# A fused decoder layer in fp32: the down projection of its MLP by seven block products for eight, half of the weight sums made by GpSimd

## The chip, the core and the metric

The kernel runs on one NeuronCore of one Trainium2 chip. The metric is the device time of one execution in microseconds; the kernel before takes 2036.14 us (median of 3 runs, 2035.08 to 2038.41). The profile holds one execution. TensorE (PE) multiplies and writes to PSUM; VectorE (DVE), ScalarE (ACT) and GpSimd (POOL) compute elementwise; SyncE (SP) issues most DMAs.

## The reference, cut to what matters

One layer of a hybrid decoder (attention beside a Mamba scan, then an MLP) for 256 tokens of width 2048, all in fp32. The change is in the MLP:

```
D_MODEL = 2048; SEQ = 256; D_FF = 4 * D_MODEL
        hn = rms_norm(h, norm_mlp_w[l])
        h = h + jnp.square(jax.nn.relu(hn @ w_up[l])) @ w_down[l]
    return rms_norm(h, norm_final_w)
```

## The kernel before, in words

**Precision.** Every large product is made of fp32r products: a weight block `raw` is split into a high part `hi` (a copy to fp32r) and a low part `lo = raw - hi`; the activations are split likewise (`LAh`/`LAl`, `LBh`/`LBl`). A block product is three matmuls of 512 columns: high by high, high by low, low by high (lines 307 to 309).

**Tiles.** Weights come in tiles of 256 rows of depth by 512 columns, so two 128x512 blocks, 512 KB in one DMA. A *chunk* is 512 output columns: 8 tiles over a depth of 2048, and for both halves of the tokens (t = 0, 1) 8 x 2 x 2 x 3 = 96 matmuls into two PSUM banks `acc[par][t]`, `par` alternating from chunk to chunk. One tile is 12 matmuls.

**The ring.** `raw`, `hi` and `lo` are rings of 4 slots (`RING`). In `load_group`, SP loads tile g once `lo` of tile g-4 is made. In `split_hi` ScalarE makes `hi` once the tile has landed and TensorE is through with tile g-4; in `split_lo` VectorE makes `lo` from it; TensorE waits for `lo` in `mm_group`. `slots` sets the order on ScalarE and VectorE: at slot s they split tile s+3 (`LEAD`), then do what is hooked to slot s. All engines work in order.

**The MLP** runs in 4 phases. Phase i makes four up chunks (columns of `w_up`; product, relu, square; transposed on VectorE by `turn_blocks`, spread by four DMAs that GpSimd issues in `spread_blocks`, and split into `LAh`/`LAl` by `act_split_s` and `dve_split_s` 4 slots after the chunk's end), and then multiplies these 2048 hidden values by a quarter of `w_down` in four down chunks, each added to the residual `H` by `add_residual`. So a phase is 64 tiles, and the MLP 256. The last chunk (`mm_last`) does its second half token half by token half, and the final norm follows: row sums, the power -1/2 on GpSimd (line 814), scaling on VectorE and ScalarE, four output DMAs.

Of the kernel before, what the change touches and what calls it, by code (L numbers as in the profile page):

```python
# [22 lines left out]
F32 = mybir.dt.float32  # L23
F32R = mybir.dt.float32r
# [7 lines left out]
P = 128  # L32
# [41 lines left out]
C_END = C_MLP + 32  # L74
# [21 lines left out]
def build(nc, a, out):  # L96
    ctx = ExitStack()
    with ctx:
# [60 lines left out]
        s_x0 = sem("first_rows_of_x_split")  # L159
        s_smw = sem("small_weights_landed")  # L160
# [81 lines left out]
        s_fr = sem("final_rsqrt_ready")  # L242
        s_fin = [[sem(f"output_ready{t}{n}") for n in range(2)] for t in range(2)]
        s_wf = sem("final_weights_landed")
        s_out = sem("output_stored")

# [50 lines left out]
        def mm_group(pe, g, par, j, Lh, Ll, n=NC):  # L297

            sl = g % RING if isinstance(g, int) else j % RING
            pe.wait_ge(s_lo, g + 1)  # L300
            for kk in range(2):
                k = 2 * j + kk
                for t in range(2):
# [213 lines left out]
        XDT = sb("XDT", [P, 2, NC], c=post)  # L517
# [4 lines left out]
        ZT = sb("ZT", [P, 2, NC], c=post)  # L522
        TB = sb("TB", [P, 2 * NC], c=post)
        YT = sb("YT", [P, NC], c=post)
        TS = W[:, 0:4, :, :].rearrange("p h c l -> p (h c l)")
        TSS = (TS, XTOK[:, :, :].rearrange("p t n -> p (t n)"))
        TBS = (TB[:, :], W[:, 4:8, :, :].rearrange("p h c l -> p (h c l)"))
        post.close()
        flat_th = TH.rearrange("p a s -> p (a s)")
# [21 lines left out]
        PART = ((slice(0, 1024), slice(1024, D)), (slice(0, 1280), slice(1280, D)))  # L551
# [8 lines left out]
        def _(sp):  # L560
# [4 lines left out]
            load_group(sp, C_KC, 0, w_in, 0, KC0)  # L565
            load_x(1)
            load_group(sp, C_KC, 1, w_in, 0, KC0)
# [3 lines left out]
            load_group(sp, C_KC, 4, w_in, 0, KC0)  # L571
            load_x(3)
            for j in (5, 6, 7):
                load_group(sp, C_KC, j, w_in, 0, KC0)
# [32 lines left out]
            with sp.Fori(0, 4) as i:  # L607
                for k in range(4):
                    load_chunk(sp, C_MLP + 8 * i + k, w_up, 0, D * i + NC * k)
                for k in range(4):  # L610
                    load_chunk(sp, C_MLP + 8 * i + 4 + k, w_dn, KT * i, NC * k)
            for t, n in ((0, 1), (0, 0), (1, 0)):
                sp.wait_ge(s_fin[t][n], 1)
                sp.dma_start(out_rows[:, t, PART[t][n]], GB[:, t, PART[t][n]]).then_inc(s_out, 16)
            sp.wait_ge(s_out, 64)
# [3 lines left out]
        def _(pool):  # L619
# [10 lines left out]
            pool.memset(identf[:, :], 0.0)  # L630
            pool.memset(zz[:, :], 0.0)
# [10 lines left out]
            pool.drain()  # L642
            pool.affine_select(identf[:, :], identf[:, :], [[-1, P]], ALU.not_equal, 1.0, base=0, channel_multiplier=1)
# [174 lines left out]
        def _(pe):  # L818
            pe.wait_ge(s_const, 1)
# [1156 lines left out]
```

## Time and profile before

| | |
|---|---|
| median of 3 runs | 2036.14 us |
| the profiled execution's own time | 2037.86 us |
| its span, first to last instruction | 2036.1 us |
| TensorE busy | 2018.9 us (99%) |
| VectorE / ScalarE / GpSimd busy | 68% / 51% / 14% |
| mean granted TensorE clock | 0.998 |
| read from HBM | 379.91 MB |

A matmul's record is longer than its share of the time, since matmuls are pipelined: what one costs is the time of a busy stretch divided by their number. "Idle before <-X" tells what ended an engine's idle time.

### The profile page before, as it was taken

How to read it: one execution, taken by the hardware profiler on the slowest of the kernel's cores; microseconds unless marked ns; L12 is line 12 of the kernel's file. 1: busy time of each engine (PE TensorE's matmuls, PEld its weight loads, DVE VectorE, ACT ScalarE, POOL GpSimd, SP SyncE). 2: the span in 40 equal slices, each digit the busy share in tenths (PEclk: the TensorE clock that was granted, in tenths of full speed). 3: DMA queues.
4: the chain of work that ended last, by engine and by line, in shares of the span. 5: the costliest groups of instructions: out<-in, count | busy, mean ns of one | idle time of the engine just before them, and what ended most of it. 6: DMA issues, size and time to landing. Idle time of an engine off the chain costs nothing.

```text
span 2036.1 us, 26601 instructions
## 1 busy us (share of the span) xinstructions
PE 2018.9 (99%) x9378; PEld 1666.9 (82%) x9378; DVE 1384.1 (68%) x1735; ACT 1034.7 (51%) x1454; POOL 278.6 (14%) x417
## 2 busy tenths in 40 slices
PE   9999999999999999999999999999999999999997
PEld 7888888888888877888887888888888888888886
DVE  6665878687665678885688877666556556655664
ACT  5444546464544567663566644544344434433443
POOL 4000111111110233330033311011001000000000
PEclk9999999999999999999999999999999999999999
DMA  8757666666666666666666677766666666666663
GB/s 274 219 178 208 195 194 191 195 192 192 175 208 208 183 191 198 193 197 209 183 185 185 194 255 233 229 211 204 215 195 203 223 197 193 221 205 185 219 216 135
DMA packets 202726, 411.49 MB, mean 202 GB/s; under 512 B 15264, under 2 KB 15360, under 8 KB 201200
## 3 DMA queue, kind: packets, MB, share of 16 engines
q1 hardware_dynamic: 188656, 364.56, 58.0%
q0 software_dynamic: 13776, 44.96, 7.6%
q8 instruction: 74, 1.21, 0.3%
q14 instruction: 44, 0.36, 0.1%
q10 hardware_dynamic: 176, 0.40, 0.1%
HBM read 379.91 MB, written 2.16 MB: 188 GB/s over the span
## 4 chain that ended last, share of the span: by engine, by line
PE 91%; DVE 3%; ACT 2%; issue 2%; ACTq 1%; DVEq 0%; POOLq 0%; POOL 0%; DMA 0%
PE acc L307 28%; PE acc L309 28%; PE acc L308 28%; DVE lo L274 1%; PE x L999 1%; ACT hi L268 1%; ACT W L1313 1%; PE tr L948 1%; PE tr L342 1%; PE x L931 1%; DVE XCT L1697 0%; PE x L937 0%; PE x L867 0%; ACTq L1314 0%; PE tr L950 0%
## 5 line engine op out<-in xcount | busy, mean ns | idle before, releaser
L274 DVE TENSOR_TENSOR lo<-raw,hi 128x1024 fp32r<-128x1024 f32 x688 | 837.8, 1233 | 457.9 <-ACT hi L268 450.0
L268 ACT ACTIVATE hi<-raw 128x1024 fp32r<-128x1024 f32 x688 | 718.8, 1057 | 623.3 <-PE acc L309 561.4
L307 PE MATMUL acc<-hi,LAh 128*128 128x512 f32 x1840 | 727.9, 396 | 0.0
L309 PE MATMUL acc<-hi,LAl 128*128 128x512 f32 x1840 | 717.3, 390 | 0.0
L308 PE MATMUL acc<-lo,LAh 128*128 128x512 f32 x1840 | 716.6, 389 | 0.0
L307 PEld LDWEIGHTS acc<-hi,LAh 128*128 128x128 f32 x1840 | 345.5, 188 | 75.3 <-issue 3.2
L309 PEld LDWEIGHTS acc<-hi,LAl 128*128 128x128 f32 x1840 | 345.3, 188 | 73.1
L308 PEld LDWEIGHTS acc<-lo,LAh 128*128 128x128 f32 x1840 | 345.6, 188 | 70.6 <-issue 1.1
L307 PE MATMUL acc<-hi,LBh 128*128 128x512 f32 x896 | 349.8, 390 | 0.0
L309 PE MATMUL acc<-hi,LBl 128*128 128x512 f32 x896 | 348.7, 389 | 0.0
L308 PE MATMUL acc<-lo,LBh 128*128 128x512 f32 x896 | 348.6, 389 | 0.0
L307 PEld LDWEIGHTS acc<-hi,LBh 128*128 128x128 f32 x896 | 168.2, 188 | 35.1 <-DVE lo L274 0.3
L309 PEld LDWEIGHTS acc<-hi,LBl 128*128 128x128 f32 x896 | 168.2, 188 | 35.0
L308 PEld LDWEIGHTS acc<-lo,LBh 128*128 128x128 f32 x896 | 168.2, 188 | 34.8
L390 POOL DMA_DIRECT2D W<-TB x48 | 26.0, 560 | 491.6 <-DVE TB L381 491.6
L1697 DVE SCALAR_TENSOR_TENSOR XCT<-XCT,CWs 128x255 f32<-128x255 f32 (+2 forms) x144 | 59.8, 477 | 0.0
L769 POOL TENSOR_TENSOR ZT<-ZT,XR 128x512 f32<-128x512 f32 x32 | 56.4, 1780 | 17.9 <-ACT ZT L1300 13.9
L390 POOL DMA_DIRECT2D XTOK<-W x48 | 26.0, 558 | 219.9 <-DVE W L381 219.9
L1211 ACT ACTIVATE PB<-x,NM 128x256 f32<-128x256 f32 (+1 forms) x64 | 26.0, 420 | 38.1 <-DVE SCB L1640 27.1
L1105 ACT ACTIVATE XR<-acc,RSX 128x512 f32<-128x512 f32 x28 | 19.3, 690 | 47.9 <-PE acc L309 46.2
L762 POOL DMA_DIRECT2D XCT<-TB x32 | 18.0, 572 | 166.2 <-DVE TB L1812 166.2
L1313 ACT ACTIVATE W<-W,NAs 128x128 f32<-128x128 f32 x128 | 39.0, 388 | 0.0
(343 smaller groups left out, 1324.4 us busy)
## 6 DMA issues: line engine op xcount, KB each, us to landing
raw<-w_in SPq DMA_DIRECT2D x304, 512.0 KB, 4.3
raw<-w_up SPq DMA_DIRECT2D x128, 512.0 KB, 3.9
raw<-w_down SPq DMA_DIRECT2D x128, 512.0 KB, 4.8
raw<-w_proj_ssm SPq DMA_DIRECT2D x64, 512.0 KB, 4.7
raw<-w_proj_nsa SPq DMA_DIRECT2D x32, 512.0 KB, 4.7
raw<-w_out SPq DMA_DIRECT2D x32, 512.0 KB, 5.5
W<-acs_rows POOLq DMA_DIRECT2D x8, 1024.0 KB, 6.7
W<-TB POOLq DMA_DIRECT2D x48, 128.0 KB, 4.1
```

Of the source, the lines that this page charges most:

```text
L268: act.activation(hi[:, sl, :, :], raw[:, sl, :, :], ACT.Copy).then_inc(s_hi, 1)
L274: dve.tensor_tensor(lo[:, sl, :, :], raw[:, sl, :, :], hi[:, sl, :, :].bitcast(F32), ALU.subtract).then_inc(s_lo, 1)
L307: pe.matmul(o, xh, wh, start=(k == 0), stop=False)
L308: pe.matmul(o, xh, wl, start=False, stop=False)
L309: x = pe.matmul(o, xl, wh, start=False, stop=(k == KT - 1))
L342: x = pe.transpose((banks or TR)[b][:, (ct % 2) * S + t * P:(ct % 2) * S + (t + 1) * P], src[:, t, ct * P:(ct + 1) * P], identf[:, :])
L390: eng.dma_start(TSS[n % 2][:, S * a:S * (a + 1)], TBS[n % 2][32 * a:32 * (a + 1), :].rearrange("i (b n) -> i b n", b=4)).then_inc(s_sp[n % ...
L769: pool.tensor_tensor(ZT[:, t, :], ZT[:, t, :], ZR[:, t, :], op)
L931: pe.matmul(X6[:, :], Q[:, n, P:S], K[:, :, 0:2 * P].rearrange("p k (b n) -> p b k n", b=2), start=(p_ == 0), stop=(p_ == 2), skip_group_c ...
L1211: act.activation(o, src, ACT.Exp, scale=SCALE, bias=NM[:, k:k + 1], accum_out=SUM[:, k:k + 1])
L1313: act.activation(W[:, h, c, :], W[:, h, c, :], ACT.Relu, bias=NAs[:, c, h:h + 1], scale=-1.0)
L1697: dve.scalar_tensor_tensor(XC[:, ct, k:S], TH[:, ct, 0:S - k], CWs[:, 3 - k, ct:ct + 1], XC[:, ct, k:S], ALU.mult, ALU.add)
```

## The change

**The seven products.** The change takes two neighbouring down chunks (c, c+1) together, with the two token halves and two neighbouring 128-row blocks of depth. That is a 2x2 by 2x2 block product, made by seven block products for eight from sums of blocks (Winograd's form of Strassen's scheme). It does so on the first four depth blocks, two units (u = 0, 1), of each chunk pair: in both pairs of phases 0 to 2 and in the first pair of phase 3, 7 pairs and 14 units. The rest stays as it was.

**The tiles of a unit.** `a` is the tile of chunk c, `b` that of chunk c+1. Two more tiles are not loaded but made in ring slots: `p` = (b0-a0, b1-b0) by VectorE, and `q` = (p1+a0, a1-q0) by GpSimd (`later_weight_sums`). All four are split into `hi` and `lo` (of `b` only the second block). TensorE does 2, 1, 2 and 2 block products on them, 21 matmuls where 24 were. A pair of chunks is 20 tiles in `QUAD_ORDER`: four plain tiles (depth 2 to 5) of chunk c, a b p q of unit 0, two plain tiles, a b p q of unit 1, six plain tiles of chunk c+1. Four products go to PSUM banks of their own (`B1`, `B5`, `B6`, `B7`), which VectorE adds up in five steps hooked to tiles 13 to 17. Per phase VectorE also makes four sums of activation blocks (`row_sums`), which ScalarE and VectorE split.

**Waits.** SP loads into the slot of an `a` or `p` only when GpSimd's sums of that unit are made (`s_wq`). VectorE makes `p` when `a` and `b` have landed. The loops over phases are written out.

**Start and tail.** The identity is made first, TensorE starts on it earlier, the first tile is split by halves, the loads of x and of the first tiles are in another order, and `turn_x(1)` stands after the first tile's matmuls. In the tail the power -1/2 is a square root on ScalarE, then a reciprocal, one Newton step and a product on VectorE, and rows t = 1 go out in four DMAs for two.

```
+QUAD_ORDER = ([("n", 0, j) for j in (2, 3, 4, 5)] + [(c, 0, 0) for c in "abpq"] + [("n", 0, j) for j in (6, 7)] +
+              [(c, 0, 1) for c in "abpq"] + [("n", 1, j) for j in (2, 3, 4, 5, 6, 7)])
...
+            def load_tile(sp, i, x):
...
+                kind, c, j, _ = tile_of(i, x)
+                if kind in "pq":
+                    return
+                sp.wait_ge(s_lo, G_MLP + PHASE * i + x - RING + 1)
+                before, _, u, _ = tile_of(i, x - RING) if x >= RING else ("n", 0, 0, 0)
+                if before in "ap":
+                    sp.wait_ge(s_wq, 4 * i + 2 * ((x - RING - UP) // QUAD) + u + 1)
...
+            def later_weight_sums(i, q, u):
...
+                pool.wait_ge(s_lo, g)
+                pool.wait_ge(s_raw[sa], 16 * (2 * C_MLP + 16 * i + tile_of(i, x)[3]))
+                pool.wait_ge(s_wt, 4 * i + 2 * q + u + 1)
+                pool.tensor_tensor(raw[:, sq, 0, :], raw[:, sp_, 1, :], raw[:, sa, 0, :], ALU.add)
+                pool.drain()
+                pool.tensor_tensor(raw[:, sq, 1, :], raw[:, sa, 1, :], raw[:, sq, 0, :], ALU.subtract).then_inc(s_wq, 1)
...
+            def seven_products(g, u, p0, p1):
...
+                pe.wait_ge(s_lo, g + 1)
+                product(B1, *rows(0, 0), g, 0, one, two)
+                product(acc[p0][0], *rows(0, 1), g, 1, False, two).then_inc(s_mm, 1)
+                pe.wait_ge(s_lo, g + 2)
+                product(acc[p1][0], *sums(4), g + 1, 1, one, False).then_inc(s_mm, 1)
+                pe.wait_ge(s_lo, g + 3)
+                product(B5, *sums(1), g + 2, 0, one, two)
+                product(B7, *sums(3), g + 2, 1, one, two).then_inc(s_mm, 1)
+                pe.wait_ge(s_lo, g + 4)
+                product(B6, *sums(2), g + 3, 0, one, two)
+                product(acc[p0][1], *rows(1, 1), g + 3, 1, False, two).then_inc(s_mm, 1)
...
+            def split_tile(i, x):
...
+                if kind in "pq":
+                    act.wait_ge(s_wt if kind == "p" else s_wq, 4 * i + 2 * ((x - UP) // QUAD) + u + 1)
+                else:
+                    act.wait_ge(s_raw[sl], 16 * (2 * C_MLP + 16 * i + loads))
+                act.wait_ge(s_mm, g - RING + 1)
+                k0 = 1 if kind == "b" else 0
+                act.activation(hi[:, sl, k0:2, :], raw[:, sl, k0:2, :], ACT.Copy).then_inc(s_hi, 1)
...
+                if kind == "a":
+                    dve.wait_ge(s_lo, g - 1)
+                    for n in (sa, sb_):
+                        dve.wait_ge(s_raw[n], 16 * (2 * C_MLP + 16 * i + tile_of(i, x + (n == sb_))[3]))
+                    for kk, (m, mk) in enumerate(((sa, 0), (sb_, 0))):
+                        y = dve.tensor_tensor(raw[:, sp_, kk, :], raw[:, sb_, kk, :], raw[:, m, mk, :], ALU.subtract)
+                    y.then_inc(s_wt, 1)
+                dve.wait_ge(s_hi, g + 1)
```

**The order on VectorE** in the down projection of phase 0. Before, from the split of the last up chunk's values (L415) on; `lo<-raw,hi` is the low part of a tile, L1872 adds a chunk to the residual:

```order
L415 TENSOR_TENSOR LAl<-XTOK,LAh 128x1024
L274 TENSOR_TENSOR lo<-raw,hi 128x1024 x4
L1872 TENSOR_TENSOR BCT<-acc,BCT 128x512 x2
L274 TENSOR_TENSOR lo<-raw,hi 128x1024 x8
L1872 TENSOR_TENSOR BCT<-acc,BCT 128x512 x2
```

In the changed kernel the second chunk pair reads so up to its unit 1 and its first steps of adding up (L2113 makes `p`, the 128x512 row is `b`, `tr` and `x` are the added banks):

```order
L2113 TENSOR_TENSOR raw<-raw 128x512 x2
L2117 TENSOR_TENSOR lo<-raw,hi 128x1024
L2117 TENSOR_TENSOR lo<-raw,hi 128x512
L2117 TENSOR_TENSOR lo<-raw,hi 128x1024 x4
L2113 TENSOR_TENSOR raw<-raw 128x512 x2
L2117 TENSOR_TENSOR lo<-raw,hi 128x1024
L2117 TENSOR_TENSOR lo<-raw,hi 128x512
L2117 TENSOR_TENSOR lo<-raw,hi 128x1024 x5
L2141 TENSOR_TENSOR BCT<-acc,BCT 128x512 x2
L2117 TENSOR_TENSOR lo<-raw,hi 128x1024
L2148 TENSOR_TENSOR BCT<-tr,BCT 128x512
```

The sums of `p` stand in front of the low part of `a`, and between the two units are only p, q and two plain tiles.

**The order on GpSimd**, changed kernel, at the end of a phase's spreads; before, each spread was followed by the next one:

```order
L426 DMA XTOK<-W 128x1x256 [waits event_read_by_dve,blocks_turned]
L426 DMA XTOK<-W 128x1x256 x3
L881 TENSOR_TENSOR raw<-raw 128x512 [waits weight_sums_made,raw0,lo_done]
L883 TENSOR_TENSOR raw<-raw 128x512
L881 TENSOR_TENSOR raw<-raw 128x512 [waits weight_sums_made,raw2,lo_done]
L883 TENSOR_TENSOR raw<-raw 128x512
```

**The order on SP**, changed kernel, the second chunk pair of a phase; before, each load waited for `lo_done` alone. The waits for GpSimd's sums (`later_weight_sums_made`) stand at the loads into the slots of `a` and `p`, and the loads behind them are held back too:

```order
L666 DMA raw<-w_down 128x2x512 [waits lo_done] x9
L666 DMA raw<-w_down 128x2x512 [waits later_weight_sums_made,lo_done]
L666 DMA raw<-w_down 128x2x512 [waits lo_done]
L666 DMA raw<-w_down 128x2x512 [waits later_weight_sums_made,lo_done]
L666 DMA raw<-w_down 128x2x512 [waits lo_done]
L666 DMA raw<-w_down 128x2x512 [waits later_weight_sums_made,lo_done]
L666 DMA raw<-w_down 128x2x512 [waits lo_done]
L666 DMA raw<-w_down 128x2x512 [waits later_weight_sums_made,lo_done]
```

Over the whole program TensorE's matmuls of 512 columns go from 8320 to 8278, which is 42 fewer, 3 for each of the 14 units.

## Rows read from the trace of the kernel before

**Rows 1.** The page: span and engines; busy us (share) xinstructions.
```profile
span 2036.1 us, 26601 instructions
...
PE 2018.9 (99%) x9378; PEld 1666.9 (82%) x9378; DVE 1384.1 (68%) x1735; ACT 1034.7 (51%) x1454; POOL 278.6 (14%) x417
```

**Rows 2.** Busy time by stretch, two MLP phases and more (us, PE, PEld, DVE, ACT, POOL, clock).
```profile
1600.00:2000.00 400.00, 400.00 (x1766) 331.23 (x1765) 233.96 (x211) 170.32 (x172) 17.33 (x32) 1.00 0.66 207
```

**Rows 3.** Waits from 1600 us on: who for whom, total us, times, longest.
```profile
ACT hi L268 <- PE acc L309: 179.9, 117, 2.0
```

**Rows 4.** Timeline in a down projection, start and length in us; then its loads.
```profile
1800.55 1.23 DVE L274 TENSOR_TENSOR lo<-raw,hi 128x1024 fp32r<-128x1024 f32 x1 [1.50 <-ACT hi L268]
...
1801.94 27.57 SPq L255 DMA_DIRECT2D raw<-w_down  x11
1801.98 0.39 PE L307 MATMUL acc<-hi,LAh 128*128 128x512 f32 x1
...
1802.18 1.06 ACT L268 ACTIVATE hi<-raw 128x1024 fp32r<-128x1024 f32 x1 [1.66 <-PE acc L309]
...
1803.27 1.23 DVE L274 TENSOR_TENSOR lo<-raw,hi 128x1024 fp32r<-128x1024 f32 x1 [1.49 <-ACT hi L268]
...
DMA to landing us min/median/max: 4.5/4.5/4.9
```

**Rows 5.** Loads of `raw`: 400 us, then a single one after an idle queue.
```profile
DMA to landing us min/median/max: 3.5/4.6/8.1
...
DMA to landing us min/median/max: 3.7/3.7/3.7
```

**Rows 6.** Group by form: a sum of two 128x512 operands on VectorE.
```profile
L1788 DVE TENSOR_TENSOR Y<-Y,XDT 128x512 f32<-128x512 f32 x8 | 5.5, 693 | 0.6
```

**Rows 7.** GpSimd sums of 128x512 (ns min/median/max), and VectorE beside two pairs.
```profile
L769 POOL TENSOR_TENSOR ZT<-ZT,XR x32: 1292/1742/2280, 702.4 to 1157.6; 128x512 f32<-128x512 f32 x32
...
909.55 3.53 POOL L769 TENSOR_TENSOR ZT<-ZT,XR 128x512 f32<-128x512 f32 x2 [1.79 <-ACT ZT L1300]
913.58 3.97 POOL L769 TENSOR_TENSOR ZT<-ZT,XR 128x512 f32<-128x512 f32 x2 [0.50 <-issue]
...
L274 DVE TENSOR_TENSOR lo<-raw,hi x3: 2311/2317/2317, 911.8 to 916.3; 128x1024 fp32r<-128x1024 f32 x3
```

**Rows 8.** Timeline from the end of an up projection, per engine.
```profile
1894.72 0.69 ACT L1105 ACTIVATE XR<-acc,RS 128x512 f32<-128x512 f32 x1 [1.66 <-PE acc L309]
...
1906.84 1.06 ACT L405 ACTIVATE LAh<-XTOK 128x1024 fp32r<-128x1024 f32 x1 [2.91 <-DMA XTOK<-W]
...
1909.08 2.35 DVE L274 TENSOR_TENSOR lo<-raw,hi 128x1024 fp32r<-128x1024 f32 x2
```

**Rows 9.** Timeline of the start.
```profile
4.42 2.18 PE L897 MATMUL x<-identf 128*128 128x128 f32 x9
...
6.39 1.91 PE L342 MATMUL tr<-identf,GA 128*128 128x128 f32 x8
...
9.17 1.65 PE L342 MATMUL acc<-identf,GA 128*128 128x128 f32 x8
...
10.74 0.47 PE L307 MATMUL acc<-hi,LAh 128*128 128x512 f32 x1
...
13.57 1.04 PE L342 MATMUL tr<-identf,GA 128*128 128x128 f32 x8
```

**Rows 10.** Timeline of the tail, and a one-column operation on ScalarE.
```profile
2026.93 0.15 DVE L1938 TENSOR_SCALAR VV<-SS 128x1 f32<-128x1 f32 x1
2027.75 0.89 DVE L1947 TENSOR_SCALAR GB<-GB,RS 128x1280 f32<-128x1280 f32 x1 [0.67 <-POOL RS L814]
...
4.18 0.20 ACT L1115 ACTIVATE SS<-mhalf 128x1 f32<-128x1 f32 x1 [1.59 <-POOLq L654]
```

**Rows 11.** Stretches behind the last matmul: the third number from the end is the granted clock.
```profile
2025.30:2027.69 2.39, 0.00 (x0) 0.00 (x0) 1.61 (x4) 0.73 (x2) 0.52 (x1) 1.00 0.72 290
2027.70:2036.00 8.30, 0.00 (x0) 0.00 (x0) 0.89 (x1) 0.94 (x1) 0.02 (x1) 0.50 0.32 127
```

More of the change, by code:

```diff
@@ L73, with tile_of @@
 C_END = C_MLP + 32
-C_END = C_MLP + 32
+UP, QUAD, TWO = 32, 20, 16
+PHASE = UP + 2 * QUAD
+G_MLP = 8 * C_MLP
+G_END = G_MLP + 3 * PHASE + UP + QUAD + TWO
+QUAD_ORDER = ([("n", 0, j) for j in (2, 3, 4, 5)] + [(c, 0, 0) for c in "abpq"] + [("n", 0, j) for j in (6, 7)] +
+              [(c, 0, 1) for c in "abpq"] + [("n", 1, j) for j in (2, 3, 4, 5, 6, 7)])
+TWO_ORDER = [("n", c, j) for c in range(2) for j in range(8)]
+def tile_of(i, x):
+    if x < UP:
+        return "n", x // 8, x % 8, x // 4 + 1
+    q, y = divmod(x - UP, QUAD)
+    order = TWO_ORDER if (q == 1 and i is LAST) else QUAD_ORDER
+    kind, c, j = order[y]
+    loads = UP // 4 + 4 * q + sum(order[z][0] not in "pq" for z in range(y % 4, y + 1, 4))
+    return kind, 4 + 2 * q + (c if kind == "n" else 0), j, loads
+LAST = 3
 E_U, E_KC, E_VC, E_AT = 0, 4, 5, 6
@@ L570, in _ @@
             load_group(sp, C_KC, 3, w_in, 0, KC0)
[L571 removed]
             load_x(3)
[L573 removed]
+            for j in (4, 5, 6, 7):
                 load_group(sp, C_KC, j, w_in, 0, KC0)
@@ new lines, in mlp_chunk, with product @@
+            def mlp_chunk(g, par, Lh, Ll, need):
+                for j in range(8):
+                    for (se, v) in need.get(j, ()):
+                        pe.wait_ge(se, v)
+                    mlp_group(g + j, par, j, Lh, Ll, t_first=(j == 0, j == 0), last=(j == 7))
+            def product(o, xh, xl, g, kk, start, stop):
+                sl = g % RING
+                pe.matmul(o[:, :], xh, hi[:, sl, kk, :], start=start, stop=False)
+                pe.matmul(o[:, :], xh, lo[:, sl, kk, :], start=False, stop=False)
+                return pe.matmul(o[:, :], xl, hi[:, sl, kk, :], start=False, stop=stop)
@@ L1397, in mlp @@
                 if first:
                     hk[4] = [lambda: act_split_s(act, 7, LBh, 12, COLS[:, CN2 + 12:CN2 + 16])]
-                slots(act, split_hi, C, 64, hk, last)
+                phase_slots(i, hk)
             mlp(0, first=True)
-            with act.Fori(1, 3) as i:
+            for i in range(1, 3):
                 mlp(i)
-            mlp(3, last=True)
+            act.wait_ge(s_v, 1)
+            act.activation(RSX[:, 2:3], VV[:, 0:1], ACT.Sqrt)
+            mlp(LAST)
             for t in range(2):
```

322 lines of the change are left out of this document (251 added, 71 removed).

## The prediction, made before the changed kernel had run

> **What bounds the kernel now.** I read the page's head and its table of busy time first: TensorE is busy for 2018.9 of 2036.1 us [rows 1]. The view by stretch shows the same for the MLP: 400.00 us busy in 400 us at a granted clock of 1.00, the upper of its two levels (2.4 GHz), with 1766 matmuls, so 0.2265 us each and 2.72 us for a tile of 12 [rows 2]. The list of waits says who runs ahead: ScalarE, which makes the high parts, waited 179.9 us for TensorE to free a ring slot [rows 3]. So the suppliers have slack, and a matmul less is 0.2265 us less, for as long as they keep it.
>
> Then the timeline, for the loop of a ring slot, which is what the change works on. TensorE begins its next tile at 1801.98; the slot it left is rewritten from 1802.18 by ScalarE (0.20 us later), and VectorE's low part starts at 1803.27 (1.09 later). For the slot before, the low part starts at 1800.55 and SP issues the next load at 1801.94 (1.39 later). That load lands 4.5 us on [rows 4]. So SP issues a load 0.20 + 1.09 + 1.39 = 2.7 us after TensorE left the slot, and it lands at 7.2. It is wanted at 11.1, when TensorE has done the four tiles of the ring (10.9) and ScalarE comes round to the slot: 3.9 us to spare.
>
> **What is removed.** 42 matmuls x 0.2265 = 9.5 us [rows 2], all on the path.
>
> **What is added beside it.** VectorE adds up the four product banks: from product tile 13 on it has nine operations of 0.69 at the most, which follow each other every 0.61 (the slot length of back-to-back ones, as two sums next to each other in the unit below), and one of 1.14, 6.6 us, beside five low parts at 1.14, 5.7 us; with drains some 13 us, where TensorE takes 5 x 2.72 = 13.6. It starts with three tiles ready. I cost it, and the four activation sums per phase, at nothing; the cover is those three tiles, 8.2 us, and beyond them it costs microsecond for microsecond. ScalarE has over a microsecond idle per tile. The unrolled loops add no wait that I can see.
>
> **What is added in a chain.** This is the term that decides. In a unit two of the four slots hold sums, so loads come late. Let A be the moment when TensorE starts on tile `a` of unit 0. It then has 21 matmuls, two plain tiles (24) and 21 matmuls: 66 x 0.2265 = 14.95 us until it wants the first plain tile of chunk c+1, and 60 (13.6 us) until `q` of unit 1. The suppliers:
> 1. Slot of the last plain tile before `a` is free at A. `q` of unit 0 gets its high part from A+0.20, its low part from A+1.29, and `b` of unit 1, whose slot it is, is issued at A+2.7 [rows 4].
> 2. It lands 4.5 us later, A+7.2 [rows 4].
> 3. VectorE, next in line, makes `p`: two sums of 0.69, 1.3 together [rows 6]: A+8.5.
> 4. GpSimd makes `q` in two sums. Alone one takes 1.29; behind a low part 2.27 or so; the median is 1.74, and a drain between them costs 0.50. Two such pairs took 3.53 and 3.97, and low parts beside them 2.32 for 1.23 [rows 7]. Each engine waits out the other's operation. I take 4.1, nearest to a first sum behind `a`'s low part (2.3), the drain (0.5) and a second alone (1.3): A+12.6.
> 5. High and low part of `q`, 1.09 + 1.28: A+14.95. TensorE wanted it at 13.6: 1.4 us late.
> 6. SP, held by GpSimd's sums, issues the next plain tile at A+12.75. The queue is idle then, where a load took 3.7; in the busy queue it took 4.6 in the median [rows 5]. I take 4.0: A+16.75. High and low part, 2.37: A+19.1.
> TensorE wanted that tile at 14.95, so it has stood still for 4.15 us in all.
>
> In the first pair of each phase it is worse. ScalarE and VectorE must split the last up chunk's values at tile 3 of the pair, ahead of `q`. The chunk ends 0.20 before 1894.72, at 1894.52; ScalarE waits for the spread values until 1906.84, and the next low part starts only at 1909.08 [rows 8]. A is 48 matmuls after the chunk's end, 1905.39, so the load of step 1 goes out at 1909.08 + 1.39 = A+5.1 instead of A+2.7: 2.4 us more, 6.55.
>
> So four first pairs lose 26.2 us and three second pairs 12.5: 38.7, less 9.5 saved, **+29.1 us**. GpSimd's part is 4.1 of a pair's chain. A sum of two such operands takes VectorE 0.69 [rows 6]: two, with a drain, would be 1.4, and 2.7 us a pair, 19 us in all, would not be lost. The Trainium skill (GPSIMD Engine Reference, Engine selection) speaks against the change here: it puts elementwise sums on VectorE, with GpSimd about twice as slow for two inputs. By its factor alone the pair of sums would take some 2.8 us and a drain, 3.3, and the result would be 6 us less; I stay with the rows, which show the two engines waiting for each other.
>
> **Start and tail.** The transposes of x start at 6.39 behind a warm-up that could end a microsecond earlier, and the first product is at 10.74; but a second block of transposes, hidden before at 9.17, now stands between products, where such a block costs 1.04 [rows 9]. I take 0.5 us saved, between 1.8 saved and 0.8 lost. In the tail the variance's start to scaling is 2026.93 to 2027.75, 0.82 us. After the variance's own 0.15 come now a root on ScalarE (0.20) and four one-column steps on VectorE at 0.15 and a drain each, some 0.7 us more [rows 10]; the last DMAs are smaller, which I take to give 0.2 back: 0.5 lost, between 0.3 saved and 1.0 lost. Together nothing.
>
> **The sum.** 2037.9 (the profiled execution, 1.7 over the median shown) + 29.1 = 2067; the median gives 2036.1 + 29.1 = **2065**.
>
> **Bounds.** Below: both loads at the shortest seen, 3.5 [rows 5], and GpSimd without meeting VectorE, 1.29 + 0.50 + 1.29 = 3.1, give 1.0 + 0.5 + 1.0 = 2.5 less a pair, 17.5 us in all: 2047.6. Above: both loads at 4.9 [rows 4] and 4.5 for GpSimd (3.97 + 0.50) give 1.7 more a pair, 12 us, and start and tail 1.8: 2079.
>
> **Rivals.**
> *The clock falls in the new gaps.* For: TensorE's gap before the plain tile is 2.7 us (16.4 to 19.1), and after the last matmul the clock stayed at 1.00 for 2.4 us and then went to 0.50, the lower level (1.2 GHz) [rows 11]. At the start the work ran at the lower level from 4.42 until past 9.17: eight transposes took 1.91 at 6.39, 1.65 at 9.17 and 1.04 at 13.57 [rows 9]. Such a stretch of 5 to 6 us at half speed costs 3, in 7 pairs 21: 2086. Against: 2.7 us is just about what the tail shows without a fall, and the gap is surrounded by full work. The Trainium skill (TensorE: Matmul & The Clock Gate, HAM oscillation) describes just this, waits for data between bursts that bring the lower clock back every time; by it the time would be that 2086.
> *VectorE becomes the bound while adding up.* If its nine operations take 1.0 for 0.69 and drains add up, it falls behind its three tiles of cover; 2 us a pair, 14 us: 2079. Against: 8 us of cover.
> *The chain fits, and it is faster.* If steps 1 to 6 end within 14.95 us, no stall is left and 9.5 us are gained: 2026.6. It turns to a gain below a chain of 16.3 (9.5 / 7 = 1.36 us of stall a pair), 2.8 us under my 19.1. For: a load has 3.9 us to spare before the change. Against: even the lower bounds of steps 2, 4 and 6 together give 16.6 in the second pairs, and 2.4 more in the first. A run near 16.3 would be no change.
> That the change does not do what it says is ruled out by the order of instructions: 42 matmuls are gone.
>
> **The chances.** My forecast 0.72 (its own range 2048 to 2079), the clock 0.10, VectorE 0.06, no stall 0.08, near balance 0.04. The 8 in 10 range goes from the lower bound towards the first two rivals: 2047 to 2082. A measurement of this kernel tells 0.2%, 4 us, from no change: faster by more 0.08, within 0.04, slower by more 0.88.
>
> **What would show it.** TensorE's idle time in the down projections, about 39 us, in gaps before `q` and before the first plain tile behind unit 1, ended by the low parts (L2117). VectorE waiting for a landing before L2113. GpSimd's pairs L881/L883 taking about 4 us, and the load waiting on them. A clock of 1.00 throughout. Wrong would be: no gaps there; gaps at the adding up; gaps at unit 0's `q` alone; or a clock of 0.50 behind them.

## The result, and the profile after

The changed kernel takes 2082.69 us in the median of four runs (2079.52 to 2084.47), the kernel before 2036.39 beside it: a ratio of 1.0225 with a 95% interval of 1.0213 to 1.0238, so 46.3 us slower. The forecast was 2065, so +29.1, with a range that ended at 2082: the sign was right, and the size was missed by 17 us. One execution of run 1 below took 4483.6 us, over twice as long as any other, and is left out. The profiled execution took 2082.11 us. Its page, against [rows 1]:

```profile
span 2080.4 us, 25990 instructions
...
PE 2028.5 (98%) x9351; PEld 1665.8 (80%) x9351; DVE 1498.1 (72%) x1877; ACT 1066.2 (51%) x1492; POOL 332.7 (16%) x443
```

The span grew by 44.3 us. TensorE is busy for longer than before although 42 matmuls are gone, which points to matmuls at the lower clock. The view by stretch shows them: the first row is the 600 us that answer to [rows 2], where before no idle time was shown; the others are the five stretches of the MLP at the lower level (us, busy us and instructions of PE, PEld, DVE, ACT and POOL, granted clock, DMA share, GB/s).

```profile
1400.00:2000.00 600.00, 565.52 (x2423) 459.38 (x2422) 430.14 (x414) 263.64 (x263) 81.25 (x82) 0.98 0.60 190
```

```profile
1435.30:1445.50 10.20, 8.07 (x18) 5.93 (x19) 6.69 (x7) 3.81 (x4) 2.04 (x1) 0.50 0.57 203
1500.20:1503.60 3.40, 3.13 (x7) 2.51 (x8) 3.06 (x4) 2.41 (x3) 0.00 (x0) 0.50 0.84 276
1626.50:1629.90 3.40, 3.40 (x10) 2.66 (x9) 2.82 (x4) 1.48 (x2) 0.79 (x1) 0.51 0.04 13
1687.90:1691.30 3.40, 3.40 (x10) 2.62 (x9) 2.90 (x4) 1.85 (x3) 0.00 (x0) 0.50 0.98 304
1998.50:2001.90 3.40, 3.40 (x10) 2.66 (x9) 2.99 (x5) 1.09 (x2) 1.16 (x1) 0.50 0.02 6
```

TensorE stands idle for 34.5 of these 600 us. In the five stretches matmuls start 0.427 apart where they otherwise start 0.2265 apart, as here in the third:

```profile
1627.16 0.63 PE L1167 MATMUL acc<-lo,LAh 128*128 128x512 f32 x1
1627.58 0.63 PE L1168 MATMUL acc<-hi,LAl 128*128 128x512 f32 x1
```

49 matmuls begin inside them (the 55 in the rows count those that reach into a stretch too), each 0.20 longer: 9.8 us for the clock. The list of waits of TensorE from 1400 us to the end (who for whom, us in total, times, longest) says what it waits for, and two more rows of that list what stands behind it; before, TensorE had no such wait, and ScalarE's longest entry was [rows 3]:

```profile
PE acc L1166 <- DVE lo L2117: 23.6, 13, 2.6
PE tr L1181 <- DVE lo L2117: 8.9, 4, 3.9
PE x L1181 <- DVE lo L2117: 3.0, 4, 1.3
...
ACT hi L1549 <- POOL raw L883: 24.7, 8, 5.0
...
POOL raw L883 <- issue: 8.8, 4, 4.3
```

`acc L1166` is the first plain tile behind a unit, `tr L1181` is the product with `q` of unit 0, `x L1181` a product with `p`. A matmul is shown with 0.39 but the next may follow after 0.2265, so a gap from start to start is 0.16 longer than its idle time. Counted from start to start, and without the clock's part, the gaps in the MLP add up to 42.4 us; my forecast had 38.7.

One first pair in full, phase 1, from the timeline (start, length, engine, line, idle before and its releaser). Tile `a` of unit 0 starts at A = 1616.3: the chunk ends 0.20 before the ACT row below, and four plain tiles, 10.9, follow.

```profile
1605.64 0.69 ACT L1537 ACTIVATE XR<-acc,RS 128x512 f32<-128x512 f32 x1 [1.66 <-PE acc L1168]
...
1610.88 2.17 POOL L426 DMA_DIRECT2D XTOK<-W  x4 [19.59 <-DVE W L417]
...
1611.62 1.28 DVE L2113 TENSOR_TENSOR raw<-raw 128x512 f32<-128x512 f32 x2
```

```profile
1613.07 2.71 POOL L881 TENSOR_TENSOR raw<-raw 128x512 f32<-128x512 f32 x1
...
1617.26 1.90 POOL L883 TENSOR_TENSOR raw<-raw 128x512 f32<-128x512 f32 x1 [1.48 <-issue]
1619.19 1.06 ACT L1549 ACTIVATE hi<-raw 128x1024 fp32r<-128x1024 f32 x1 [2.69 <-POOL raw L883]
1619.23 0.88 SPq L666 DMA_DIRECT2D raw<-w_down  x2
...
1621.56 0.51 PE L1181 MATMUL tr<-hi,LSh 128*128 128x512 f32 x1 [1.68 <-DVE lo L2117]
...
1625.84 0.47 PE L1166 MATMUL acc<-hi,LAh 128*128 128x512 f32 x1 [2.61 <-DVE lo L2117]
```

```profile
1627.64 1.29 DVE L2113 TENSOR_TENSOR raw<-raw 128x512 f32<-128x512 f32 x2 [0.58 <-DMA raw<-w_down]
...
1629.11 2.11 POOL L881 TENSOR_TENSOR raw<-raw 128x512 f32<-128x512 f32 x1 [9.95 <-DVE raw L2113]
...
1631.37 1.56 POOL L883 TENSOR_TENSOR raw<-raw 128x512 f32<-128x512 f32 x1
1633.00 0.37 SPq L666 DMA_DIRECT2D raw<-w_down  x1
```

```profile
1639.37 0.50 PE L1166 MATMUL acc<-hi,LAh 128*128 128x512 f32 x1 [1.34 <-DVE lo L2117]
```

Three things are to be seen. GpSimd's pair in unit 1 takes from 1628.93, the end of VectorE's sums, to 1632.93: 4.0 us. In unit 0, right behind the DMAs that spread the last up chunk's values, the first sum is 2.71, then GpSimd waits 1.48 for nothing that the profile shows (4.33 in phase 0), and from the end of VectorE's sums at 1612.90 it is 6.26 us. And SP issues no load at all between 1603.54 and 1619.23: the first of the next four, into the slot of `a`, waits for GpSimd, and the other three queue behind it. Their landings, from that line's own view for 1619 to 1622 us:

```profile
L666 SPq DMA_DIRECT2D raw<-w_down x4: 367/391/468, 1619.2 to 1621.5; - x4
...
DMA to landing us min/median/max: 4.1/5.5/6.0
```

### The profile page after: what moved, and what is told of

Its sections match the earlier page's. It is cut to its first block, busy times and chain, and to the rows that moved or that the text cites. A ratio compares the mean times of both kernels' runs of the same rounds, so it can differ in the third digit from the quotient of the medians.

```text
span 2080.4 us, 25990 instructions
## 1 busy us (share of the span) xinstructions
PE 2028.5 (98%) x9351; PEld 1665.8 (80%) x9351; DVE 1498.1 (72%) x1877; ACT 1066.2 (51%) x1492; POOL 332.7 (16%) x443
## 4 chain that ended last, share of the span: by engine, by line
PE 83%; DVE 4%; DMA 4%; ACT 2%; issue 2%; POOLq 2%; POOL 1%; DVEq 0%; ACTq 0%; SPq 0%
PE acc L343 17%; PE acc L345 17%; PE acc L344 17%; PE acc L1166 9%; PE acc L1168 9%; PE acc L1167 8%; DMA raw<-w_down 3%; POOLq L882 1%; DVE lo L307 1%; DVE lo L2117 1%; POOL raw L883 1%; ACT hi L1549 1%; PE x L1077 1%; DMA raw<-w_in 1%; PE tr L1026 1%
## 5 line engine op out<-in xcount | busy, mean ns | idle before, releaser
L307 DVE TENSOR_TENSOR lo<-raw,hi 128x1024 fp32r<-128x1024 f32 x434 | 532.2, 1240 | 269.4 <-ACT hi L301 262.5
L301 ACT ACTIVATE hi<-raw 128x1024 fp32r<-128x1024 f32 x434 | 452.2, 1057 | 333.6 <-PE acc L345 274.5
L1549 ACT ACTIVATE hi<-raw 128x1024 fp32r<-128x1024 f32 (+1 forms) x281 | 290.2, 1037 | 327.7 <-PE acc L1168 230.9
L2117 DVE TENSOR_TENSOR lo<-raw,hi 128x1024 fp32r<-128x1024 f32 (+1 forms) x281 | 351.5, 1271 | 138.1 <-ACT hi L1549 135.3
L343 PEld LDWEIGHTS acc<-hi,LAh 128*128 128x128 f32 x1344 | 252.8, 188 | 59.9 <-issue 6.9
L345 PEld LDWEIGHTS acc<-hi,LAl 128*128 128x128 f32 x1344 | 252.6, 188 | 54.2
L344 PEld LDWEIGHTS acc<-lo,LAh 128*128 128x128 f32 x1344 | 253.0, 188 | 51.4 <-issue 1.4
L1166 PE MATMUL acc<-hi,LBh 128*128 128x512 f32 x512 | 199.3, 389 | 0.0
L1166 PE MATMUL acc<-hi,LAh 128*128 128x512 f32 x384 | 154.6, 403 | 23.7 <-DVE lo L2117 23.6
L1166 PEld LDWEIGHTS acc<-hi,LBh 128*128 128x128 f32 x512 | 96.1, 188 | 20.2 <-DVE lo L2117 0.4
L1167 PEld LDWEIGHTS acc<-lo,LBh 128*128 128x128 f32 x512 | 96.1, 188 | 20.0
L1168 PEld LDWEIGHTS acc<-hi,LBl 128*128 128x128 f32 x512 | 96.1, 188 | 20.0
```

The lines of the kernel that those rows point to most:

```text
L301: act.activation(hi[:, sl, :, :], raw[:, sl, :, :], ACT.Copy).then_inc(s_hi, 1)
L307: dve.tensor_tensor(lo[:, sl, :, :], raw[:, sl, :, :], hi[:, sl, :, :].bitcast(F32), ALU.subtract).then_inc(s_lo, 1)
L343: pe.matmul(o, xh, wh, start=(k == 0), stop=False)
L344: pe.matmul(o, xh, wl, start=False, stop=False)
L345: x = pe.matmul(o, xl, wh, start=False, stop=(k == KT - 1))
L1166: pe.matmul(o, xh, wh, start=(kk == 0 and t_first[t]), stop=False)
```

## The experiments

Each batch had its own runs of the kernel before (medians 2035.4 to 2036.4). The ratios are each against its own batch. The last but one column is the idle time that the profile shows on TensorE from 1400 to 2000 us.

| run | median us | ratio to before (95%) | against before | PE idle | clock |
|---|---|---|---|---|---|
| the change | 2082.7 | 1.0225 (1.0213, 1.0238) | +46.3 | 34.5 | 0.992 |
| start_tail | 2035.3 | 0.9995 (0.9985, 1.0005) | -0.7 | | |
| q_on_dve | 2052.0 | 1.0079 (1.0062, 1.0095) | +16.0 | 17.1 | 0.999 |
| gaps_filled | 2075.6 | 1.0201 (1.0183, 1.0218) | +39.5 | (filled) | 0.998 |
| spread_on_act | 2075.7 | 1.0186 (1.0169, 1.0203) | +39.6 | 34.2 | 0.995 |
| sums_warmed | 2072.2 | 1.0175 (1.0160, 1.0191) | +35.8 | 29.3 | 0.994 |
| q_dve_late_split | 2048.9 | 1.0063 (1.0048, 1.0079) | +12.5 | 15.1 | 0.999 |
| order_pool | 2079.1 | 1.0212 (1.0196, 1.0228) | +42.7 | 32.0 | 0.993 |
| order_dve | 2049.1 | 1.0059 (1.0046, 1.0073) | +12.7 | 15.7 | 0.998 |
| warmed_filled | 2063.9 | 1.0136 (1.0119, 1.0153) | +28.5 | (filled) | 0.999 |
| q_dve_low_first | 2045.7 | 1.0043 (1.0027, 1.0060) | +10.3 | 13.4 | 0.998 |
| ring_apart_pool | 2044.7 | 1.0044 (1.0028, 1.0059) | +8.8 | 11.1 | 0.997 |
| ring_apart_dve | 2027.1 | 0.9958 (0.9944, 0.9972) | -8.8 | 0.0 | 0.999 |

**1. Start and tail alone.** The kernel before with the changed start (warm-up, split first tile, order of the x blocks) and the changed tail (root on ScalarE, finer last stores), and none of the down projection:

```
-            split_hi(act, C_KC, 0)
+            act.activation(hi[:, 0, 0, :], raw[:, 0, 0, :], ACT.Copy).then_inc(s_g0h, 1)
+            act.activation(hi[:, 0, 1, :], raw[:, 0, 1, :], ACT.Copy).then_inc(s_hi, 1)
...
-                dve.wait_ge(s_fr, t + 1)
+                root_inverse(t)
```

> The kernel before with the changed start and tail alone; the MLP is as before. Theory (the loss is in the down projections; from the changed kernel's trace the start costs 2.0 us and the tail gives 1.8 back): 2036, between 2034.5 and 2038. Rival (start and tail hold a part of the 17 us by which the forecast fell short): 2041 or more.

Measured 2035.3 in the median of ten executions, no difference. The only trace of this kernel is of the one that is left out, so no stretch of it is read here. By the interval, -3.1 to +1.0 us, the whole of the 46 us is in the down projections.

**2. All four sums on VectorE.** GpSimd's two sums go into the same place on VectorE's queue, behind its own two:

```
+                    dve.drain()
+                    dve.tensor_tensor(raw[:, sq, 0, :], raw[:, sp_, 1, :], raw[:, sa, 0, :], ALU.add)
+                    dve.drain()
+                    dve.tensor_tensor(raw[:, sq, 1, :], raw[:, sa, 1, :], raw[:, sq, 0, :], ALU.subtract).then_inc(s_wq, 1)
```

> The changed kernel with all four weight sums on VectorE, none on GpSimd. Theory (the chain from load to load through GpSimd's sums makes the gaps): the chain is 2.5 to 3 us shorter a pair and unit 0 of the first pairs no longer waits 6.3 us for its sums: stalls of 42 us fall to 15 to 25, most clock falls go too: 2050 to 2062. Rival (VectorE's own load makes the gaps): VectorE has 2.6 us a pair more to do, so no faster than the changed kernel, 2080 or more.

Measured 2052.0: GpSimd as the maker costs 30 us of the 46, directly and through the clock, which now never falls in the MLP. TensorE's waits (same columns as above) are shorter, none over 1.5, but they are still there, and with the 9.5 saved they are why it stays slower than before:

```profile
PE acc L1163 <- DVE lo L2119: 12.3, 11, 1.5
PE tr L1178 <- DVE lo L2119: 4.8, 7, 0.9
```

**3. Gaps filled.** In the changed kernel TensorE transposes an identity, 7 to 19 times, where it would stand still:

```
+                if q == 0 and one:
+                    fill(p1, 13)
                 pe.wait_ge(s_lo, g + 4)
                 product(B6, *sums(2), g + 3, 0, one, two)
```

> The changed kernel with small transposes of the identity (0.13 us each, results never read) in TensorE's gaps: 13 before q of unit 0 and 19 before the next plain tile in first pairs, 10 before chunk c+1; in second pairs 7 before p of unit 1 and 19 before chunk c+1. Theory (the clock falls because of these gaps and costs 9.6 us in the MLP): no falls there, the stalls stay, 2071 to 2076. Rival (the falls have another cause, or the stalls alone hold the loss): 2081 or more.

Measured 2075.6, 7.1 less, with the same suppliers. One fall of 3.4 us was left, in phase 0, where the gap is longest and the filling was too short for it. So the lower clock costs real time, and the gaps themselves stayed. How much, this run shows only roughly: of the 7.5 us between the two profiled executions 4.6 stand ahead of the MLP (its first row work begins at 1348.0 for 1352.7), and the MLP itself, from there to the last matmul, took 715.0 for 718.2. Run 9 below is the cleaner test.

**4. The spread off GpSimd's queue.** The last spread of each phase is issued on ScalarE's queue:

```
-                for n in range(4 * i, 4 * i + 4):
+                for n in range(4 * i, 4 * i + 3):
...
+                hk[33] = [lambda: spread_blocks(act, 8 + 4 * i + 3, E_MLP + 4 * i + 2, s_spx)]
```

> The changed kernel, but the last spread of each phase is issued on ScalarE's queue, so that GpSimd issues no DMA just before unit 0's sums. Theory A (the DMA work queued on GpSimd is what stretches unit 0's two sums to 6.3 us): they take about 4 us, the gap of 2.8 us before the plain tile in first pairs falls under 1, with the clock falls behind it: 2070 to 2077. Theory B (they are long because VectorE's operations lock GpSimd out): 6 us as before, 2080 to 2085.

Measured 2075.7. The first sum was 2.11 instead of 2.71, but the pause stayed, 1.15 and 4.01 in phase 0, though GpSimd had issued its last DMA more than 21 us before. In GpSimd's timeline:

```profile
1612.02 2.11 POOL L882 TENSOR_TENSOR raw<-raw 128x512 f32<-128x512 f32 x1 [21.77 <-DVE raw L2116]
1615.28 1.69 POOL L884 TENSOR_TENSOR raw<-raw 128x512 f32<-128x512 f32 x1 [1.15 <-issue]
```

Unit 0's pair came down from 6.26 to 5.12 us: in phases 1 to 3 the queue was half of the surcharge over 3.98, in phase 0 (8.49 to 7.58) a fifth of it, and the pause was something else.

**5. GpSimd's first drain taken early.** As 4, and before it waits for the first unit GpSimd makes a tiny sum, a drain and a tiny difference on a scratch tile:

```
+                pool.tensor_tensor(TW[:, 0:2], TW[:, 0:2], TW[:, 2:4], ALU.add)
+                pool.drain()
+                pool.tensor_tensor(TW[:, 4:6], TW[:, 0:2], TW[:, 2:4], ALU.subtract)
+                pool.drain()
```

> The changed kernel with the last spread of each phase issued on ScalarE's queue (as in spread_on_act), and before GpSimd waits for the first unit of a phase it makes a tiny addition, a drain and a tiny subtraction on a scratch tile. Theory A: the pause between GpSimd's two sums in unit 0 of first pairs (1.15 us, 4.01 in phase 0, against 0.14 in the other units) is the fetching of code for the drain or the subtraction, which GpSimd no longer has at hand after it has issued DMAs; done once on the scratch tile in its idle time, the pause falls to 0.1 to 0.3 us, the pair of sums to 4.0 us, TensorE's gaps shrink by about 1.0 us in three phases and 3.9 in phase 0, and the time falls from 2075.7 to 2064 to 2070 us. Theory B: the pause comes from what VectorE and the DMA engines do beside the first unit; then the scratch operations change nothing, the pause stays at 1.1 and 4.0, and the time is 2073 to 2078 us.

The pause went to 0.14 in 13 of the 14 pairs (0.45 in one), phase 0's too. The rows are those of the scratch drain, which took over the waiting, and of the drain between the real sums (ns, min/median/max); in spread_on_act the same drain had a maximum of 6062:

```profile
L892 POOLq DRAIN  x4: 7197/7808/8622, 1399.0 to 1952.1; - x4
```

```profile
L885 POOLq DRAIN  x14: 2186/2192/2234, 1421.5 to 1988.1; - x14
```

So the surroundings (theory B) are out: it is the first drain behind DMA issues on GpSimd that is slow, and it can be had in idle time. Idle time alone does not do it: in the change GpSimd waited up to 29.5 us before a later unit, and the pause there was 0.14. Whether that is the fetching of code, as theory A said, is not shown; a scratch drain of 7.2 us or more right behind the issues, against a pause of 4.0 at the most 22 us behind them, could as well be work left over from the DMAs. The time, 2072.2, is 2 us above what theory A gave, and TensorE's clock fell six times in this kernel's MLP (20.5 us at the lower level), where run 4's had three stretches (13.7 us): idle gaps of 2.2 to 2.6 us were left in each pair.

**6. The split one tile later**, with all sums on VectorE: high and low parts of the last up chunk's values are made after tile 4 of the first pair.

```
-                    hk[8 * k + 11] = [lambda k=k: act_split_s(act, 8 + k, LAh, 4 * k, later=128 * i)]
+                    hk[8 * k + 11 + 1 * (k == 3)] = [lambda k=k: act_split_s(act, 8 + k, LAh, 4 * k, later=128 * i)]
```

> The changed kernel with all four weight sums on VectorE (as in q_on_dve, 2052.0 us), and the split of the last up chunk's values one tile later, after tile 4 of the first pair instead of tile 3. Theory A (my forecast's step that the spread values hold up the load of b of unit 1 in first pairs): the first pairs' gaps, 3.2 us a pair in q_on_dve against 2.2 in second pairs, come down to those of second pairs; 4 us less, 2046 to 2050 us. Theory B: the wait only moves behind the next tile, and the gaps stay: 2050 to 2054 us.

2048.9, 3.1 less than run 2, and the two intervals overlap: what was expected, with little certainty. The idle time shown fell from 17.1 to 15.1.

**7 and 8. Four plain tiles between the units**, with the sums on GpSimd, and with them on VectorE (and the later split); the adding up moves back by two tiles:

```
-               [(c, 0, 1) for c in "abpq"] + [("n", 1, j) for j in (2, 3, 4, 5, 6, 7)])
+               [("n", 1, j) for j in (2, 3)] + [(c, 0, 1) for c in "abpq"] + [("n", 1, j) for j in (4, 5, 6, 7)])
```

> The changed kernel, sums still on GpSimd, with four plain tiles between the two units of a pair instead of two (two plain tiles of chunk c+1 are taken ahead of unit 1). Theory A (the stall is a chain of load, sums, load across two units that stand too close): unit 1's loads have 5.4 us more, its q is not late; what stays is the first plain tile behind a unit, which waits for GpSimd's sums, now behind each unit. The gap sum falls from about 42 to some 35 us and the clock falls stay where gaps are over 2.5 us: 2070 to 2080 us. Theory B (GpSimd's sums are what stalls, whatever the distance): each of the 14 units stalls by itself for 3 us or so: 2078 to 2088 us.

> Four plain tiles between the units, all four weight sums on VectorE, and the last up chunk's split one tile later. Theory A (distance and the sums' engine are the whole stall): the gaps go nearly away, and up to 9.5 us come back of 42 matmuls less: 2028 to 2040 us, with a clock of 1.00 throughout. Theory B (two of four slots hold sums, so a unit cannot be fed in time in a ring of four whatever the order): gaps of 1 to 1.5 us behind each unit, 14 to 21 us in all: 2041 to 2050 us.

2079.1 and 2049.1. The gaps before `p` and `q` of unit 1 shrank, and the gaps before the first plain tile behind each unit stayed or grew; the sum hardly moved (3.6 us less than the change, and even with run 6). Run 7's time lies in the ranges of both its theories and decides nothing; run 8 failed its theory A outright and lies in theory B. The distance between the units is not what matters. What was left standing was that theory B: a unit cannot be fed in a ring of four of which two slots hold sums.

**9. Gaps filled, and the first drain taken early**, runs 3 and 5 together (so with the spread on ScalarE's queue too), and with fewer transposes than run 3.

> sums_warmed (2072.2 us, gaps of 36.0 us on TensorE in the MLP, clock falls that cost 8.9) with transposes of an identity on TensorE in the gaps, some fewer than the gaps are long. Theory A (what is lost is the gaps plus the clock that falls behind them): the clock stays at 1.00, the gaps stay, 2036.4 less 9.5 saved and 36.0 of gaps is 2063 us; 2061 to 2066, since a transpose too many stands in the way of the next product. That is also the case that my forecast described (full clock, GpSimd's pairs at 4.1 us). Theory B (the clock figure is a reading of the trace and not time that can be had back): 2070 to 2074 us.

2063.9, in its theory A. The clock stayed at 1.00 in the whole MLP, and in the profiled executions the MLP took 702.1 us where run 5's took 711.1: 9.0 less, for 46 matmuls begun at the lower clock in run 5, 9.2 by the rows. This is the kernel that my forecast described, with that clock and every pair of GpSimd at 4.0: +28.5 us, forecast +29.1.

**10. The low part of `a` first**, on VectorE, ahead of the four sums (based on run 6):

```
+                dve.wait_ge(s_hi, g + 1)
+                dve.tensor_tensor(lo[:, sl, k0:2, :], raw[:, sl, k0:2, :], hi[:, sl, k0:2, :].bitcast(F32),
+                                  ALU.subtract).then_inc(s_lo, 1)
                 if kind == "a":
...
-                dve.wait_ge(s_hi, g + 1)
```

> q_dve_late_split (2048.9 us) with VectorE making the low part of tile a before the four sums instead of behind them. In that kernel the gap of 1.4 us before the first plain tile behind a unit comes of its load, which is issued right behind the low part of a that follows the sums. Theory A: in second pairs the low part then fits into the wait for the landing of b, the next load goes out some 0.7 us earlier, and the gaps fall by 0.5 to 1 us in six or seven of the 14 units: 2043 to 2047 us. Theory B: VectorE is busy without a pause there, what is put first puts the sums back by as much, and p and q come late instead: 2048 to 2052 us.

2045.7, 3.2 less than run 6, with intervals that overlap; in the trace the gaps before `q` are gone. The gaps behind units, 0.9 to 1.9 of idle time, stayed. Their load still goes out only when the unit's sums are made: in phase 1, unit 1, VectorE's last sum ends at 1615.61, SP issues at 1615.68, and it lands 4.35 us later.

**11 and 12. `p` and `q` out of the ring.** The sums go to buffers of their own, in `GB`, which is idle in the MLP until the last phase's second pair, and the four slots of `raw` hold loaded tiles alone. The loads into the slots of `a` and `b` still wait for the unit's sums, but two more are under way while a unit is worked on:

```
-                        y = dve.tensor_tensor(raw[:, sp_, kk, :], raw[:, sb_, kk, :], raw[:, m, mk, :], ALU.subtract)
+                        y = dve.tensor_tensor(PQ[u][0][:, kk, :], raw[:, sb_, kk, :], raw[:, m, mk, :], ALU.subtract)
...
-                sp.dma_start(raw[:, x % RING, :, :], src).then_inc(s_raw[x % RING], 16)
+                sp.dma_start(raw[:, load % RING, :, :], src).then_inc(s_raw[load % RING], 16)
```

> The changed kernel, with the sums p and q written into buffers of their own (two sets, in a part of SBUF that is idle during the MLP) instead of into two of the four slots that the loads use; the four slots now hold loaded tiles alone, and GpSimd still makes q. Theory A (my forecast's main step: the stall is that two of four slots hold sums, so the loads behind a unit go out late): the gaps before the first plain tile behind each unit (1.5 to 2.8 us each in the changed kernel) and before q of unit 1 go; what stays is the gap before q of unit 0 in first pairs (1.85, 4.07 in phase 0), where GpSimd's own 6.3 to 8.5 us decide. 9.5 saved, 8 to 14 of gaps, 3 to 5 for the clock: 2036 to 2046 us. Theory B (GpSimd's time is the stall, and the loads only hide behind it): the gaps before q grow by what the others lose, and the time stays over 2060 us.

> The same buffers of their own for p and q, with all four sums on VectorE and the last up chunk's split one tile later (as in q_dve_late_split, 2048.9 us). Theory A (VectorE as the maker of the sums, and slots held by them, are the whole stall): nearly no gap is left in the MLP, the 42 matmuls less are 9.5 us less, and start and tail cost nothing: 2026 to 2032 us, faster than the kernel before. Theory B (VectorE itself is too full around a unit, with row work, sums and adding up): gaps of 1 us a unit stay, 2036 to 2042 us.

Run 11 differs from the change in this alone, and takes 2044.7 for 2082.7: 38 us came back. TensorE's whole list of waits from 1400 us on:

```profile
PE tr L1186 <- DVE lo L2124: 9.3, 4, 3.9
PE x L1186 <- DVE lo L2124: 1.8, 2, 1.1
```

No wait before a plain tile is left. The four before `tr` are GpSimd's slow first pairs, as in the change (8.9); its timeline in phase 1 shows them much as they were (6.33 us for 6.26), while SP now has a load out from 1596.81 on, beside them, and not behind:

```profile
1596.81 12.53 SPq L670 DMA_DIRECT2D raw<-w_down  x5
...
1598.16 2.71 POOL L886 TENSOR_TENSOR GB<-GB,raw 128x512 f32<-128x512 f32 x1
...
1603.02 1.29 POOL L888 TENSOR_TENSOR GB<-raw,GB 128x512 f32<-128x512 f32 x1 [2.15 <-issue]
...
1606.72 0.50 PE L1186 MATMUL tr<-hi,LSh 128*128 128x512 f32 x1 [1.76 <-DVE lo L2124]
```

Run 12 takes GpSimd out as well. It is 8.8 us faster than the kernel before, by its interval 5.7 to 11.4, and faster than both kernels. TensorE is idle nowhere in the 600 us, and its page has 2011.6 us busy for the 2018.9 of [rows 1]:

```profile
1400.00:2000.00 600.00, 600.00 (x2637) 494.56 (x2637) 463.38 (x478) 286.50 (x295) 28.19 (x53) 1.00 0.66 208
```

```profile
PE 2011.6 (99%) x9351; PEld 1659.9 (82%) x9351; DVE 1493.6 (74%) x1905; ACT 1064.2 (53%) x1492; POOL 276.5 (14%) x415
```

## Why the prediction was right in sign and wrong in size

- **The saving, 9.5 us.** Right: run 12, in which nothing stands in its way, gains 8.8. In its profiled execution the MLP took 667.1 us for 674.1 before, 7.0 less: 9.5 less the 1.6 of small delays of the ledger below and eight of 0.1 or so.
- **Start and tail at nothing.** Right: run 1 measures -0.7 within its interval. In the profile the first row work of the MLP comes 2.0 us later (1353.4 for 1351.4) and what follows the last matmul is 1.8 shorter. The 2.0 are of this execution more than of the start: its clock fell once at 25.6 to 29.0 too, and in the twelve profiled executions with this start the first row work on ScalarE begins at 1347.6 to 1352.7, 1350.2 in the median, before at 1350.7. Inside the tail the root itself costs 1.0 more than before (from 2072.96 to 2074.78 against the 0.82 of [rows 10]), which the smaller last stores outweigh:

```profile
2072.96 0.15 DVE L2225 TENSOR_SCALAR VV<-SS 128x1 f32<-128x1 f32 x1
...
2074.78 1.02 DVE L2248 TENSOR_SCALAR GB<-GB,RS 128x640 f32<-128x640 f32 x2 [0.47 <-issue]
```

- **VectorE's adding up at nothing.** Right as far as the gaps tell: none is ended by it, and in run 12 it stands beside a TensorE without any idle time.
- **Steps 3 and 4.** Right: 1.3 for VectorE's two sums, 4.0 for GpSimd's pair (forecast 4.1) in ten of 14 units. Step 4 left out that GpSimd has issued DMAs just ahead of unit 0 in first pairs, and there it is 6.26, in phase 0 8.49.
- **Step 1: right in time, for another reason; step 2: 1.5 short.** In first pairs `b` of unit 1 was to be issued at A+5.1, because the split of the up values holds up `q`. It went out at 1621.54, A+5.2, but because `q` itself was late: GpSimd ended it at 1619.16, and its low part at 1621.51 frees the slot. SP's wait for GpSimd's sums of unit 0 stands in front of it. I had not put SP's queue at this place; it did not delay the issue of `b`, but it bunched the loads: four that go out within 2.3 us land after 4.1, 5.1, 6.0 and 6.0 us, and `b`, the last, took 6.0 for the 4.5 of step 2. The first of them is the plain tile behind unit 0, which TensorE waited for.
- **Steps 5 and 6.** Step 6 right: 4.0 us from issue to landing (1633.00 to 1636.98) and 2.4 for the parts; the tile starts at 1639.37, A+23.1 for the forecast's A+21.5, and those 1.6 us are step 2's. Step 5's order was wrong: the forecast had nothing before unit 1, and three quarters of the gaps of this first pair (4.6 of 6.1) stand there, before `q` of unit 0 and the tile behind it. By the sum they were accounted for all the same: 1.85 + 2.78 + 1.51 = 6.1 us of gaps in this pair, forecast 6.55; 4.3 in the pair behind it (0.29, 1.43 and 2.58), forecast 4.15. All gaps are 42.4, forecast 38.7, and phase 0's pause, 4.33 where the other phases have 1.48, is most of the difference.
- **The clock: the step that failed.** The sum put it at nothing; I had it among the rivals with a chance of 0.10, on the ground that the clock had held for 2.4 us behind the last matmul [rows 11] and that the gap of 2.7 stands in full work. The first ground did not carry: 2.4 us is when the clock fell there, and my gap was longer. The clock did fall. Behind the gap of 2.6 us of idle time that ends at 1625.84 it was at the lower level from 1626.5 to 1629.9, and so within 1.4 us behind two more gaps; two other falls, one of them for 10.2 us, began in the last microsecond of a gap. That is 9.8 us by the rows. By the runs it is 7.1 between the medians of the change and run 3, of which the profiled executions show only 3.1 in the MLP, with one fall left and the transposes in the way; and 8.3 between runs 5 and 9 (7.3 with each against its own kernel before), where the profiled executions show 9.0 in the MLP. So it is about 7 to 10 us. The fall does not follow from the gap's length alone: it came behind idle gaps of 2.2 to 2.6 us (run 5), of 1.8 (runs 7 and 11) and 1.9 (run 10), not behind one of 3.1 (run 4), and not once in the MLP of runs 2, 6 and 8, whose longest gap is 1.5.
- **The ledger.** From its first row work to the last matmul the MLP took 718.2 us for 674.1 before, 44.1 more: 42.4 of gaps + 9.8 for the clock - 9.5 saved + 1.6 of delays under 0.06 each between matmuls (2.1 in all, 0.5 before, and 2.1 in run 12 too), 44.3. Start and tail add 0.2 to the span, which grew by 44.3. So the forecast's +29.1 lacks 3.7 of gaps, 9.8 of clock and 1.6 of small delays, and the medians differ by 2.0 more than the spans. Without the clock's part and GpSimd's slow drains the forecast holds within a microsecond (run 9), and part of that is luck: steps 1, 2 and 5 had the right lengths for waits that stood elsewhere.

The rival that I weighed at 0.10, the clock, gave 2086 with mine for the gaps, and was the right case. Its price was not: it had 3 us in each of seven pairs, 21, and the rows show 9.8 in five stretches; it lies near 2082.7 because the gaps were too small in it. The rule of the Trainium skill (TensorE: Matmul & The Clock Gate, HAM oscillation) that I set aside there, bursts with waits for data between them that bring the lower clock back, is what these rows show, though not behind every gap. The waits in the Trainium skill's example there are 3 to 5 us, longer than all but one of the changed kernel's gaps (3.9); that about 2 us can be enough is shown by these runs, not by it. The other one that I weighed (GPSIMD Engine Reference, Engine selection), that elementwise sums belong on VectorE, was right by more than its factor of about two: the pair takes GpSimd 3.98 us from release to end, beside VectorE's low parts, and VectorE 1.54 in run 2 (1612.53 to 1614.07). Run 2 against the change is 30 us, for 14 pairs of sums, 2.2 us a pair; I had named 19 for it, since I counted the sums and neither the slow drains nor the clock.

And the mechanism that mattered most is only half named in the forecast. It said that two of four slots hold sums; it did not ask what a fifth and sixth slot would give. Run 11 gives 38 us for that, the clock's part included, with GpSimd as slow as ever, more than run 2 gives for taking GpSimd out. The two do not add: a slow maker is harmless except at its own product as long as loads do not wait for it, and the held slots cost 38 us with GpSimd's sums and 22 with VectorE's (runs 6 and 12).

## What to carry to other kernels

Before values that are computed go into the slots of a load ring, count how many loads are still under way while they stand there, and what each queue's next load waits for: a slow producer then holds up not its own product alone but every load queued behind. A supplier's delay that puts some two microseconds of idle time on TensorE can have a second price, the clock behind it (from 1.8 us on here, never up to 1.5), so cost such gaps with it from the start. And where an engine issues DMAs and computes, look at the first drain behind the issues, not only at the operations.

## What the hardware showed that I had not expected

- On GpSimd the first drain behind DMA issues took 7.2 to 8.6 us right behind them (run 5), and kept the next operation waiting 1.1 to 4.0 us even where over 20 us of idle time stood between (run 4); the later drains let the next operation start 0.14 us after the one ahead.
- GpSimd's sum of two 128x512 operands had two levels, 2.11 in most units and 2.71 right behind its own DMA issues (2.11 there too once the issues were on ScalarE, run 4); the second of a pair was 1.56, 1.90 beside a low part in unit 0, and 1.26 in phase 0, where VectorE did nothing.
- VectorE's low part took 1.98 for 1.23 where it overlapped a GpSimd sum, as at 1614.89 in the changed kernel:

```profile
1614.89 1.98 DVE L2117 TENSOR_TENSOR lo<-raw,hi 128x1024 fp32r<-128x1024 f32 x1 [0.26 <-ACT hi L1549]
```

- After a pause, loads that go out close together land 4.1 us after issue for the first and 6.0 for the fourth, where the evenly paced ones of [rows 4] took 4.5.
